# Three instead of four ordinary pairs ahead of the seven-product pairs in each feed-forward layer

## The reference

```python
def swiglu(h, w_gate, w_up, w_down):
    return (jax.nn.silu(h @ w_gate) * (h @ w_up)) @ w_down

xp = xp + swiglu(rmsnorm(xp, norm_ffn[i]), ffn_w_gate[i], ffn_w_up[i], ffn_w_down[i])
xs = xs + swiglu(rmsnorm(xs, norm_ffn[i]), ffn_w_gate[i], ffn_w_up[i], ffn_w_down[i])
```

## Time and profile before

| | us |
|---|---|
| median of three runs | 2039.98 |
| lowest, highest | 2039.18, 2043.82 |
| the profiled execution | 2047.97 |
| its span, first to last instruction | 2046.2 |
| TensorE matmul busy | 2006.8 |
| VectorE busy | 1345.7 |
| ScalarE busy | 1061.5 |
| GpSimd busy | 380.8 |

### The profile page before, as it was taken

The page is one execution under the profiler, slowest core; times in us unless marked ns, Lnnn a source line. Parts: engine busy times, 40 slices in busy tenths (PEclk is TensorE's granted clock), DMA queues, the critical chain, the costliest instruction groups (busy, mean ns, idle before and its releaser), DMA issues.

```text
span 2046.2 us, 41692 instructions
## 1 busy us (share of the span) xinstructions
PE 2006.8 (98%) x16576; PEld 1941.2 (95%) x16576; DVE 1345.7 (66%) x2268; ACT 1061.5 (52%) x1842; POOL 380.8 (19%) x397
## 2 busy tenths in 40 slices
PE   8999999999899999999999979999999999999999
PEld 7999999998599999999999859999999999999998
DVE  4994586468768945864466655885587368936852
ACT  4563465365455634653777753463365355624642
POOL 3210110169421101101111114110111120101101
PEclk8999999999999999999999999999999999999999
DMA  5363664244214636643432252363564314636642
GB/s 188 106 181 91 163 182 128 81 126 115 78 63 113 182 93 165 181 129 88 175 112 88 86 194 92 113 175 97 150 187 138 109 57 127 172 93 182 180 118 80
DMA packets 99526, 264.86 MB, mean 129 GB/s; under 512 B 13353, under 2 KB 16329, under 8 KB 99316
## 3 DMA queue, kind: packets, MB, share of 16 engines
q1 hardware_dynamic: 74756, 217.14, 32.9%
q0 software_dynamic: 24208, 44.72, 11.9%
q10 hardware_dynamic: 384, 0.55, 0.1%
HBM read 213.40 MB, written 8.60 MB: 108 GB/s over the span
## 4 chain that ended last, share of the span: by engine, by line
PE 87%; POOL 4%; DVE 4%; ACT 2%; issue 1%; DMA 1%; SPq 0%; ACTq 0%; POOLq 0%; DVEq 0%
PE acc L693 44%; PE pair L893 20%; PE acc L893 10%; PE bank L893 5%; POOL conv L2600 4%; PE pair L1095 1%; PE pair L774 1%; PE bank L1115 1%; DMA hist_rows<-in_state_pool 1%; DVE w_lo L1858 1%; PE pair L1070 1%; DVE xn L1999 1%; DVE xt L2066 0%; ACT w_hi L1328 0%; PE bank L1105 0%
## 5 line engine op out<-in xcount | busy, mean ns | idle before, releaser
L1328 ACT ACTIVATE w_hi<-raw 128x768 fp32r<-128x768 f32 (+1 forms) x220 | 199.3, 906 | 429.9 <-PE acc L693 427.6
L693 PE MATMUL acc<-h_hi,w_hi 128*128 128x260 f32 x1408 | 399.5, 284 | 0.0
L693 PE MATMUL acc<-h_lo,w_hi 128*128 128x260 f32 x1408 | 398.3, 283 | 0.0
L693 PE MATMUL acc<-h_hi,w_lo 128*128 128x260 f32 x1408 | 397.6, 282 | 0.0
L1858 DVE TENSOR_TENSOR w_lo<-raw,w_hi 128x768 fp32r<-128x768 f32 (+1 forms) x220 | 240.9, 1095 | 216.4 <-ACT w_hi L1328 211.0
L693 PE MATMUL acc<-xin_hi,w_hi 128*128 128x260 f32 x1152 | 332.6, 289 | 6.0 <-DVE w_lo L1858 4.8
L693 PE MATMUL acc<-xin_hi,w_lo 128*128 128x260 f32 x1152 | 326.2, 283 | 0.0
L693 PE MATMUL acc<-xin_lo,w_hi 128*128 128x260 f32 x1152 | 325.6, 283 | 0.0
L693 PEld LDWEIGHTS acc<-h_hi,w_hi 128*128 128x128 f32 x1408 | 265.2, 188 | 0.6
L693 PEld LDWEIGHTS acc<-h_hi,w_lo 128*128 128x128 f32 x1408 | 265.1, 188 | 0.0
L693 PEld LDWEIGHTS acc<-h_lo,w_hi 128*128 128x128 f32 x1408 | 264.8, 188 | 0.0
(11 more groups left out here) (442 smaller groups left out, 5377.8 us busy)
## 6 DMA issues: line engine op xcount, KB each, us to landing
raw<-in_ffn_w_gate SPq DMA_DIRECT2D x88, 512.0 KB, 3.6
raw<-in_ffn_w_up SPq DMA_DIRECT2D x88, 512.0 KB, 4.5
raw<-in_ffn_w_down SPq DMA_DIRECT2D x64, 384.0 KB, 3.2
raw<-in_ffn_w_down SPq DMA_DIRECT2D x64, 320.0 KB, 2.9
w_sum<-in_ffn_w_up SPq DMA_DIRECT2D x72, 256.0 KB, 4.8
raw<-raw POOLq DMA_DIRECT2D x72, 256.0 KB, 3.4
w_sum<-raw POOLq DMA_DIRECT2D x72, 256.0 KB, 4.1
raw<-in_attn_w_qkv SPq DMA_DIRECT2D x24, 512.0 KB, 3.6
```

Source lines behind the costliest of these rows:

```text
L693: last = pe.matmul(acc[:, b, 0:HALF], w[:, w_tile * P:(w_tile + 1) * P], v[:, h * HALF:(h + 1) * HALF], start=start and t == 0, stop=stop ...
L1328: act.activation(w_hi[n.slot(2)][:, 0:cols], raw[:, q.slot(4), 0:cols], ACT.Copy).then_inc(split_hi, 1)
```

## The change

Three pairs per layer are ordinary and nineteen are made in sevens: eight in the first half, eleven in the second. VectorE's four sums of x are taken into a function `x_sum(t)`. The first two stay where they were, in pair c = 1 ahead of the up evacuation, and the low part of operand 0 follows them there. The third and the fourth, and the low parts of operands 1, 2 and 3, come at the end of that pair, behind the split of unit 5 and the low part of h. SyncE's crossed DMA waits for two sums instead of four. The program of ScalarE is not edited; its conditions on `PLAIN` give other places now.

```diff
--- before.py
+++ after.py
@@ -50,7 +50,7 @@
 
 
 FH = 11
-PLAIN = 4
+PLAIN = 3
 PAIRS_OF = (range(0, FH - PLAIN), range(FH - PLAIN, 2 * FH - PLAIN))
 PAIRS = 2 * FH - PLAIN
 LOADS, DOWN, DOWN_M = [], [], []
@@ -575,7 +575,7 @@
                     if kind == "pair" and g:
                         J = PAIRS * layer + n
                         if n < 2:
-                            sp.wait_ge(x_summed, 4 * layer + 4)
+                            sp.wait_ge(x_summed, 4 * layer + 2)
                         if J >= 2:
                             sp.wait_ge(blk_lo, 7 * (J - 2) + 5)
                         sp.dma_start(crossed(J).rearrange("p (k c) -> p k c", c=P),
@@ -1999,6 +1999,14 @@
                         last = dve.scalar_tensor_tensor(to[:, k, :], x[:, k, cols], g, rstd[:, cols], ALU.mult, ALU.mult)
                     return last
 
+                def x_sum(t):
+
+                    to, a, b, made = ((xt[:, 0], xn1[:, 0:4], xn0[:, 0:4], 0), (xt[:, 1], xn1[:, 4:8], xt[:, 0], 1),
+                                      (xt3[:], xn0[:, 4:8], xt[:, 1], 2), (xt[:, 2], xn1[:, 0:4], xn1[:, 4:8], 0))[t]
+                    if made:
+                        dve.wait_ge(x_summed, 4 * layer + made)
+                    dve.tensor_tensor(to, a, b, ALU.subtract).then_inc(x_summed, 1)
+
                 def x_low(b):
 
                     dve.wait_ge(xs_hi_ok, 7 * layer + b + 1)
@@ -2059,14 +2067,9 @@
                     if c == 1:
                         dve.wait_ge(x_scaled, layer + 1)
                         dve.wait_ge(stored, 16 * STORED[("pool0", "conv", "attn", "pool1")[layer]])
-                        for to, a, b, made in ((xt[:, 0], xn1[:, 0:4], xn0[:, 0:4], 0), (xt[:, 1], xn1[:, 4:8], xt[:, 0], 1),
-                                         (xt3[:], xn0[:, 4:8], xt[:, 1], 2), (xt[:, 2], xn1[:, 0:4], xn1[:, 4:8], 0)):
-                            if made:
-                                dve.wait_ge(x_summed, 4 * layer + made)
-                            dve.tensor_tensor(to, a, b, ALU.subtract).then_inc(x_summed, 1)
-                    if c + 2 == PLAIN:
-                        x_low(1)
-                        x_low(2)
+                        x_sum(0)
+                        x_sum(1)
+                        x_low(0)
                     dve.wait_ge(units_done, n.start + 2)
                     dve.tensor_tensor(halves(up2[:]), accumulator(At(1)), halves(rstd[:]), ALU.mult).then_inc(evacuated, 1)
                     if c + 1 == PLAIN:
@@ -2085,10 +2088,11 @@
                         for k in range(4, KT):
                             last = scaled(k)
                         last.then_inc(x_scaled, 1)
-                    if c + 3 == PLAIN:
-                        x_low(0)
                     if c + 2 == PLAIN:
-                        x_low(3)
+                        x_sum(2)
+                        x_sum(3)
+                        for b in range(1, 4):
+                            x_low(b)
 
                 def join(j, ahead, last):
```

## The result

| | before | after |
|---|---|---|
| median, lowest to highest, us | 2041.38 (2039.18 to 2047.63, 6 runs) | 2056.51 (2053.41 to 2059.31, 6 runs) |
| the profiled execution, its span | 2047.97, 2046.2 | 2058.23, 2056.2 |
| TensorE busy, matmuls | 2006.8, 16576 | 2005.9, 16528 |

The ratio of the times is 1.0064, with a 95% interval of [1.0049, 1.0079]: slower by 13.1 us, 10.0 to 16.1. The direction was right. The forecast stood on the first median of before, 2039.98; on that one the ratio gives 2053.0, inside the range of 2045.5 to 2054.5, while the measured median, 2056.51, lies 2 us above its end. The two profiled spans differ by 10.0.

The account below looks back on a forecast made before the run. TensorE, busy 98% of the span, was taken as the bound. To the median of 2039.98 us it added 9.0 for waits less the saving and 1.6 for the clock: 2050.6 us, with 8 in 10 from 2045.5 to 2054.5.

Parts of the forecast that it names:

- The saving: Per layer one ordinary pair (11.48 us) becomes one of seven blocks (10.07): 1.41 us, 5.6 over four layers.
- The wait before the first block: TensorE waits for VectorE's first low part: 2.2 us in layers 1 and 2, 3.1 in layers 0 and 3.
- The hole for ScalarE: VectorE stands still 1.56 us at unit 4's split, which ScalarE makes only after operand 0's high part.
- Rival 2: ScalarE's early high part of operand 0 costs nothing: +2.2 us in all, 2042.2 us; chance 7%.
- ScalarE's copies: In the first pair of sevens, blocks 2 and 4 wait for late bank copies: 0.46 and 0.43 us, 0.90 together.
- behind that every wait has room: After the first pair's two copy waits nothing more is lost; the next pair's first low part is 2.1 us early.
- The clock: TensorE's granted clock falls behind the two long waits, layers 0 and 3: 0.8 us net each, 1.6 in all.
- The absorption: At half rate in the first pair, the 0.90 us of waits for ScalarE vanish: 1.7 us becomes 0.8 net.
- rival 3: The clock holds at 1.00 through all four new waits: 2049.0 us; chance 25%.
- The DMAs: SyncE's crossed DMA waiting for the second sum keeps a stall away: weights at 649.9, wanted 654.1, otherwise 656.4.
- The sum: Layers 1 and 2 lose 1.7 us each, layers 0 and 3 2.8 each: +9.0, plus 1.6 for the clock.

Follow-up runs that it names:

- the first experiment: The changed kernel with ScalarE's high part of operand 0 moved behind the split of unit 4 and the silu: 2046.81 us, ratio 1.0028.
- just-in-time version: On top of the first experiment, the fourth weight sum and low parts of operands 2 and 3 between blocks' low parts, ScalarE's operand 4 earlier: 2043.15 us, ratio 1.0017.
- kept-busy version: The changed kernel with 17 or 24 unread matmuls ahead of each layer's first block, so TensorE doesn't idle: 2051.49 us, ratio 1.0037.
- the experiment on SyncE's wait: The changed kernel with SyncE's crossed DMA waiting for four sums again instead of two: 2056.97 us, ratio 1.0075.
- the GpSimd experiment: On top of the first experiment, the third and fourth sums of x made by GpSimd instead of VectorE: 2049.36 us, ratio 1.0041.

## Why the prediction was right, and by how much it missed

*The saving.* Right: 48 matmuls fewer. In the blocks' stretch a further pair costs 10.07 us, and everything beyond that is waits, below.

*The wait before the first block.* Right in mechanism and size. To the first block the change took 9.31 us less in layer 1 and 9.30 in layer 2, and an ordinary pair is 11.48: 2.17 and 2.18 lost, where I had 2.18. In layers 0 and 3, 3.32 and 3.35, where I had 3.36 and about 3.3. The hole for ScalarE is there with 1.48 us (I said 1.56), and the first experiment shows that it is worth 6.2 of the 11.4 us, or 7.0 with the clock falls that went with it. Rival 2, that it is harmless, is out. (Its sum was also too low: without the hole layers 0 and 3 still lose 3.34 - 1.56 = 1.78 us ahead of the first block, which gives +1.3 each and not +1.0.)

*ScalarE's copies.* Right for the two that I had followed, and one was put at nothing. By the distances between starts in layer 1, where the clock held, block 2 of the first pair lost 0.44 us and block 4 0.41; I had 0.46 and 0.43. The step that did not hold is "behind that every wait has room". I had looked only at the second pair's first low part. Its block 2 began 0.35 us late (670.12), when the copy at 669.71 had ended. In ScalarE's order that copy stands behind a high part of weights, for which ScalarE waits 1.77 us until VectorE has made a sum of weights. With 0.10 us for the restart behind the long wait, and less the 0.14 of loss that was already in the 70.56, that makes the 81.82 - 70.56 - 10.07 = 1.19 us that layer 1 lost, where I had 0.90. The copy for block 6 costs nothing in the change; where the first block doesn't wait, it is the next bound, as the just-in-time version shows.

*The clock.* Two falls of 0.8 us net were forecast, in the long waits; there were three, of 0.3 us each (kept-busy version against the change). The absorption was the right thought and was underrated. All falls together cost 0.9 us, so rival 3 (none, 2049.0) and my 1.6 were about equally near.

*The DMAs.* The direction was right; the stall that the edit keeps away is 1 us a layer, not 2.3, by the experiment on SyncE's wait.

*The sum.* 10.6 us predicted, 11.43 in the ramps. By layers: 3.65, 1.7, 1.7, 3.6 predicted, 3.53, 1.95, 2.39, 3.56 measured. What is missed in layer 2 is the third fall and the second pair's copy.

*The range.* Too narrow on the slow side: the change came out near its end. I added the difference to one median of three runs and allowed too little for the scatter of what lies outside the ramps. The medians of before in this study went from 2039.98 to 2041.42, and single runs of the change from 2053.4 to 2059.3. The 11.4 us of the ramps lie inside the measured interval; the medians' difference of 15.1 is 3.7 more. The clock that each run was granted on average shows what the scatter is made of. Of 28 runs of before that stand beside the first experiments, the 11 with 0.995 or more took 2035.6 to 2040.1 us, the 8 with 0.992 or less 2042.7 to 2048.0. The six runs of the change had 0.989 to 0.991. In the profiled one the three falls behind the first blocks, some 10 us at the lower rate, take 0.0025 off that mean, so in its other stretches too the clock stood where the slower runs of before have it. Whether the change brings that about or six runs met it by chance stays open; the kept-busy version, with 0.993 to 0.996, took less time, and that fits either.

## What to carry to other kernels

Taking a slow piece out of the front of a pipeline pays only if the engine that prepares the next stage has the slack; count that engine's unbroken work against the time up to its first customer, before counting what the busy engine saves. Moving work behind the first customer doesn't remove it: the versions above shifted the wait between unit 5, block 0, block 6 and the next pair, and in none did the ramps fall below those of the kernel before. And where places in a program are counted from the end (`PLAIN` less three), changing the count moves instructions that the diff doesn't show; here that was over half of the loss.

## What the hardware showed that I had not expected

In the GpSimd experiment VectorE and GpSimd shut each other out for whole instructions. In its rows the product h ends at 637.81, which is 0.55 us after GpSimd's first sum (637.26), and the split's low part ends at 641.19, 1.08 after GpSimd's second (640.11): if each ran only when GpSimd was done, it took about its usual 0.70 and 1.22 us, less 0.15 of overlap. GpSimd's second sum likewise ended 2.30 us after VectorE's h, and its first 2.31 us after the end of VectorE's low part of operand 0 (634.95). All four layers show the same durations within 0.05 us. The evacuation from PSUM at 634.86, with one SBUF input, took its usual 0.69 beside it. The Trainium skill, "SBUF — State Buffer", section "SBUF: two separate sides", describes this as an exclusive lock against VectorE's operations with two SBUF inputs; the trace agrees in all four places.

The clock is no function of the idle time before it in this range: 2.00 us ahead of 1328.03 brought a fall and 1.99 ahead of 655.95 none, with the same matmuls before and behind. In the version with ScalarE's order 2.56 us ahead of layer 3's first block brought a fall (0.50) and 2.67 ahead of layer 0's none (1.00).
